# One stage for head norm and long convolutions with a product on GpSimd, HGRN states beside the projections, and full 128-row matmuls

## The reference, cut to what matters

```python
z = v
for order, gate in enumerate((x1, x2)):
    z = gate * fft_long_conv(z, two_sided(filt[:, order, 0], filt[:, order, 1]), skip[order])
```

```python
o_inter = jnp.einsum('bhck,bhkv->bhcv', qx * jnp.exp(bx), S)
S_new = jnp.exp(b_last[:, :, 0, :])[..., None] * S + jnp.einsum('bhsk,bhsv->bhkv', kx * jnp.exp(b_last - bx), vx)
o = rms_norm_2(o, out_norm) * jax.nn.silu(g.reshape(B, T, HG_HEADS, HG_DV))
```

## Time and profile before

| | |
|---|---|
| runs (us) | 4213.64, 4215.24, 4210.41; median 4213.64 |
| the profiled execution (us) | 4211.26, of which 4209.5 are the traced span |
| mean granted TensorE clock | 0.93 |
| PE busy | 89% of the span |
| DVE, ACT, POOL busy | 49%, 21%, 34% |

### The profile page before, as it was taken

The page is one execution under the profiler, slowest core; times in us unless marked ns, Lnnn a source line. Parts: engine busy times, 40 slices in busy tenths (PEclk is TensorE's granted clock), DMA queues, the critical chain, the costliest instruction groups (busy, mean ns, idle before and its releaser), DMA issues. The chain is left out here.

```text
span 4209.5 us, 45870 instructions
## 1 busy us (share of the span) xinstructions
PE 3750.4 (89%) x18394; PEld 2959.2 (70%) x18394; DVE 2054.6 (49%) x3022; ACT 872.7 (21%) x1689; POOL 1418.6 (34%) x615
## 2 busy tenths in 40 slices
PE   7897888999989889868999898878999888888998
PEld 2683567888878588746878466757887566667887
DVE  4796443223456356654233377753133477653132
ACT  2213412100021333301100344511000243501001
POOL 1321043235553100005455222235445222144444
PEclk8998789999999799988999899989999899989999
DMA  4444212212122000103322221123322221123332
GB/s 160 140 141 156 90 40 71 66 56 66 61 62 79 23 1 1 61 0 90 100 91 80 72 70 46 36 65 90 96 89 71 83 55 46 30 80 90 95 95 70
DMA packets 400355, 306.83 MB, mean 73 GB/s; under 512 B 11228, under 2 KB 367783, under 8 KB 399560
## 3 DMA queue, kind: packets, MB, share of 16 engines
q1 hardware_dynamic: 398040, 303.37, 23.4%
q10 hardware_dynamic: 2095, 0.44, 0.1%
HBM read 297.48 MB, written 6.29 MB: 72 GB/s over the span
## 5 line engine op out<-in xcount | busy, mean ns | idle before, releaser
L400 POOL TENSOR_TENSOR low<-raw,high 128x1024 fp32r<-128x1024 f32 (+1 forms) x437 | 1062.9, 2433 | 1390.4 <-DVE high L331 1390.4
L460 PE MATMUL scores<-high 128*128 128x512 f32 (+1 forms) x2496 | 962.4, 386 | 118.4 <-POOL low L400 102.7
L460 PE MATMUL scores<-low,high 128*128 128x512 f32 (+1 forms) x2496 | 948.7, 380 | 0.0
L460 PE MATMUL scores<-high,low 128*128 128x512 f32 (+1 forms) x2496 | 946.4, 379 | 0.0
L331 DVE CAST high<-raw 128x1024 fp32r<-128x1024 f32 (+1 forms) x437 | 417.3, 956 | 689.2 <-PE scores L460 376.4
L460 PE MATMUL bank<-high 128*128 128x512 f32 (+1 forms) x1760 | 648.4, 368 | 3.4 <-POOL low L400 3.4
L460 PE MATMUL bank<-low,high 128*128 128x512 f32 (+1 forms) x1760 | 647.9, 368 | 0.0
L460 PE MATMUL bank<-high,low 128*128 128x512 f32 (+1 forms) x1760 | 647.2, 368 | 0.0
L460 PEld LDWEIGHTS scores<-high 128*128 128x128 f32 x2496 | 482.3, 193 | 224.3 <-POOL low L400 111.0
L460 PEld LDWEIGHTS scores<-high,low 128*128 128x128 f32 x2496 | 480.5, 193 | 89.8
L460 PEld LDWEIGHTS scores<-low,high 128*128 128x128 f32 x2496 | 482.3, 193 | 86.1 <-issue 0.5
(11 more groups left out here) (575 smaller groups left out, 4358.3 us busy)
## 6 DMA issues: line engine op xcount, KB each, us to landing
raw<-in_mlp_w SPq DMA_DIRECT2D x128, 512.0 KB, 4.0
raw<-in_w_in SPq DMA_DIRECT2D x76, 512.0 KB, 3.8
ring<-in_ada_w SPq DMA_DIRECT2D x32, 1024.0 KB, 7.2
raw<-in_w_gate SPq DMA_DIRECT2D x44, 512.0 KB, 3.8
raw<-in_w_up SPq DMA_DIRECT2D x44, 512.0 KB, 3.7
raw<-in_w_down SPq DMA_DIRECT2D x40, 512.0 KB, 3.3
mix<-in_ada_w SPq DMA_DIRECT2D x16, 1024.0 KB, 6.7
raw<-in_od_w_in SPq DMA_DIRECT2D x29, 512.0 KB, 3.7
```

What stands on the lines that cost most here:

```text
L400: pool.tensor_tensor(tile(low, u), tile(raw, u), tile(high, u).bitcast(F32), ALU.subtract)\
L460: mm = pe.matmul(out(p), stationary, moving, start=(k0 + k == 0 and i == 0), stop=(k0 + k == job.kc - 1 and i == len(pairs) - 1))
```

## The change

1. **hyena** becomes one stage. The 512 channels are cut in two halves, and with two orders this gives four steps k of 256 channels. PE's order is written out: turn(0), the sums of the head norm, transform(0), turn(1), transform(1), transform_back(0), turn(2), two spreads of the norm, transform(2), two more, transform_back(1), turn(3), transform(3), transform_back(2), transform_back(3). DVE does, for each k, join(k), multiply(k, 0), skip_and_gate(k-1), multiply(k, 1), with the head norm's scaling behind k = 1. `long_convolution` is gone.
2. Inside it, for each k and each group of frequencies f, **GpSimd makes one of the four products** (sine spectrum by sine filter, 128x512), DVE the other three.
3. **HgrnStates** is a side of `products`: exponentials and decays at unit 0, the chain over chunks, the squares and their sums behind unit 1, the reciprocal and the spreads at unit 2, scaling and gate at unit 3. The update of the first chunk is a copy and needs no state matmul. `w_proj_a` uses banks 6 and 7 alone. `w_proj_b`'s activations are split when the gated heads are there, at the end of unit 3 (`ready`).
4. The sums and spreads of all head norms, and those of `delta_features`, use **all 128 columns and rows**; `hy_hid` and `hy_w3` of the prologue get 128 rows, the lower 64 cleared by DVE. `ones` becomes a broadcast column of `picker`.

```diff
+        def lead(i):
+            job = jobs[raws[i][1]]
+            return 1 if job.ready is not None else AHEAD if i else 3 if job.own_room else 1
...
-                pe.matmul(m.bank[1 + i % 4][:, 0:tn], m.ident[0:n, i:i + 1].broadcast_to([n, P]),
-                          roots[0:n, 0:tn], start=True, stop=True).then_inc(spread, 1)
+                pe.matmul(m.bank[1 + i % 4][:, 0:tn], m.ident[:, i:i + 1].broadcast_to([P, P]),
+                          roots[:, 0:tn], start=True, stop=True).then_inc(spread, 1)
...
-                    hy_hid=[HY_FFN, 2, T], hy_w3=[HY_FFN, 2048], hy_not_first=[P, 2, 4],
+                    hy_hid=[P, 2, T], hy_w3=[P, 2048], hy_not_first=[P, 2, 4],
...
+        @block.gpsimd
+        def _(pool):
+            for k in range(4):
+                pool.wait_ge(joined, 8 * (k + 1))
+                if k % 2 == 0:
+                    pool.wait_ge(filters_loaded[k // 2], 16)
+                for f in range(2):
+                    n = 2 * k + f
+                    if n:
+                        pool.wait_ge(added, 2 * n)
+                    pool.tensor_tensor(parts[:, 1, :, :], spectrum(k, f)[1], filter_of(k, f)[1], ALU.mult)\
+                        .then_inc(multiplied_by_gpsimd, 1)
...
+                dve.tensor_tensor(a, uc, fs, ALU.mult).then_inc(multiplied, 1)
+                dve.wait_ge(multiplied, n + 1)
+                dve.tensor_tensor(uc, uc, fc, ALU.mult).then_inc(weighed, 1)
+                dve.wait_ge(multiplied_by_gpsimd, n + 1)
+                dve.tensor_tensor(us, us, fc, ALU.mult).then_inc(weighed, 1)
+                dve.wait_ge(weighed, 2 * n + 2)
+                dve.tensor_tensor(us, us, a, ALU.add).then_inc(added, 1)
+                dve.tensor_tensor(uc, uc, b, ALU.subtract).then_inc(added, 1)
+                for half in (1, 0):
+                    for_even, for_odd = ((ALU.add, ALU.subtract), (ALU.subtract, ALU.add))[half]
+                    low, high = spec[:, k % 2, half, f, :], spec[:, k % 2, half, 2 + f, :]
+                    dve.wait_ge(added, 2 * n + 2 - half)
+                    dve.tensor_tensor(odd[:, k % 2, 2 * f + half, :], low, high, for_odd).then_inc(differed, 1)
+                    dve.wait_ge(differed, 2 * n + 2 - half)
+                    dve.tensor_tensor(low, low, high, for_even).then_inc(folded, 1)
...
-            hgrn_states(nc, m, q, f, b, part(40, 8), i_rows, yb)
-            head_norm(nc, m, yb, HEADS, (LAT,), columns[:, 23:24], 1.0, gate=gate)
+            states = HgrnStates(m, q, f, b, part(48, 12), last, part(40, 8), i_rows, yb, columns[:, 23:24], gate)
             products(nc, m, [
...
-                    "vector", room=halves),
+                    "vector", room=halves, banks=(6, 7)),
...
-                    room=halves),
+                    room=halves, ready=states.wait_for_heads),
...
-                    written_by=1, room=halves)], ring_tiles=3, sums=SquareSums(m, x, toks))
+                    written_by=1, room=halves)], ring_tiles=3, sides=[states], sums=SquareSums(m, x, toks))
```

More of the change, by code:

```diff
@@ L370, in _ @@
                     halve_weights(dve, u + AHEAD)
[L371 removed]
+                while 0 < ahead < len(raws) and lead(ahead) == AHEAD and raws[ahead][0] <= u + AHEAD:
                     halve_activations(dve, ahead)
                     ahead += 1
+                for side in sides:
+                    side.vector_first(dve, u)
                 for p in done_in.get(u, []):
@@ L1921, in long_convolution @@
[L1921 to L1929 removed]
+    W = 256
@@ new lines, in spread_root @@
+            def spread_root(i):
+                if i == 0:
+                    pe.wait_ge(inverted, 1)
+                    pe.wait_ge(skipped, 4)
+                if i >= 2:
+                    pe.wait_ge(scaled, i - 1)
+                pe.matmul(m.bank[4 + i % 2][:, :], m.ident[:, i:i + 1].broadcast_to([P, P]), roots[:, :],
+                          start=True, stop=True).then_inc(spread, 1)
+            turn(0)
+            for i in range(4):
+                pe.wait_ge(squared, i + 1)
+                mm = pe.matmul(m.bank[4][:, :], m.row_picker(i, P), sq[:, i, :], start=(i == 0), stop=(i == 3))
@@ L1961, in _ @@
+            act.activation(roots[:, :], m.bank[4][:, :], ACT.Sqrt, **inverse_root(P)).then_inc(rooted, 1)
+            copy_odd(0)
+            for k in range(1, 4):
+                copy_turned(k)
+                copy_odd(k)
         @block.vector
         def _(dve):
-            step = Chain(dve, chain)
-            spec_of = lambda v, half, f: v[:, half, :, :].rearrange("p (side f) n -> p side f n", f=2)[:, :, f, :]
-            def join(f):
-                for half in range(2):
-                    i = 2 * f + half
-                    dve.wait_ge(copied, i + 1)
-                    even, o = m.bank[2 * i][:, :], odd[:, i, :]
-                    dve.tensor_tensor(spec[:, half, f, :], even, o, ALU.add).then_inc(joined, 1)
-                    first, second = (even, o) if half == 0 else (o, even)
-                    dve.tensor_tensor(spec[:, half, 2 + f, :], first, second, ALU.subtract).then_inc(joined, 1)
@@ L2013, in delta_features @@
+            dve.wait_ge(rooted, 1)
+            dve.reciprocal(roots[:, :], roots[:, :]).then_inc(inverted, 1)
+            for k in range(4):
+                join(k)
+                multiply(k, 0)
+                if k:
+                    skip_and_gate(k - 1)
+                multiply(k, 1)
+                if k == 1:
+                    norm_heads()
+            skip_and_gate(3)
 def delta_features(nc, m, dtb, alog, rest, beta, g, qk, v, k_rows, v_rows, loads):
```

464 lines of the change are left out of this document (296 added, 168 removed).

## The result

| | before | changed |
|---|---|---|
| runs, median (us) | 4212.02 (4209.76 to 4215.24, 4 runs) | 4147.15 (4140.49 to 4148.37, 4 runs) |
| the profiled execution, its span (us) | 4211.26, 4209.5 | 4148.37, 4146.6 |
| mean granted clock | 0.930 | 0.942 |

The ratio is 0.9842, its 95% interval 0.9825 to 0.9859: 64.9 us gained, where the prediction said 78 and kept 4104 to 4161. The kernel before was measured beside every run, and its own median moved by some us from one time to the next, so I compare ratios: those of the experiments with the mean of the two, 0.9836. 0.001 of ratio is 4.2 us. The mean has a spread of its own, some 4 us either way.

The account below looks back on a forecast made before the run. It took PE (busy 89%) as limited by engines taking turns in the convolutions and HGRN, and by half clock in few-row stretches. Savings 18 + 36 + 9 + 3 + 12 = 78 gave 4135 us, range 4104 to 4161.

Parts of the forecast that it names:

- Convolutions: Merged hyena stage: DVE and PE work side by side, 122 us becomes 98 before GpSimd's effect; 18 saved, bounds 10 and 28.
- the cold last transform: End of the convolutions: PE, idle for 8 us, starts the last back transform at half clock and loses 2 us.
- GpSimd's term: Convolutions: GpSimd's products hold up DVE's, six of eight at 1.0 us each, costing 6; bounds 0 and 10.
- the clock's 8: Convolutions, low bound: the clock falls in each of four PE gaps, at 2 us each.
- HGRN: Each second layer: HGRN runs beside the projections, so `w_proj_b` starts earlier; 18 saved per layer, bounds 12 and 21.
- the takes of unit 0 come behind them: HGRN stage: DVE's decays meet GpSimd's weight lowering and delay these takes; 0 to 4 us lost, 2 taken.
- The rival of the exclusive port: GpSimd and DVE exclude each other: 10 lost in convolutions, 4 per HGRN layer; 70 saved, 4144 us; 22%.
- Prologue: Prologue filters with full rows: the clock rises from 0.50; 12 us saved, bounds 0 and 16.
- `delta_features`: Its spreads with full rows: 22.7 us at half clock becomes 13.5, cold start of 2.2 included; 9 saved, bounds 0 and 11.
- even head norm: The even layer's norm with full rows: 10.5 us becomes 7.4; 3 saved, bounds 0 and 4.
- few rows hold the clock: The rival denied this for prologue, `delta_features` and even head norm: their 24 us fall away, 54 saved, 4160 us; 12%.
- The slow one: Merged stages: short PE bursts keep the clock at 1.2 GHz, mean near 0.55; 54 us slower, 4267; 2%.

Follow-up runs that it names:

- experiment 1: The changed kernel with the convolutions' fourth product made by DVE instead of GpSimd: 4134.15 us, ratio 0.9811.
- Experiment 2: The changed kernel with DVE's HGRN decays put behind the takes of unit 0 instead of ahead of them: 4131.66 us, ratio 0.9809.
- experiment 5: The changed kernel measured a second time, unedited, as control: 4143.22 us, ratio 0.983.
- experiments 3 and 4: The changed kernel with few rows again, in the spreads of even head norm and `delta_features` (4155.95 us, ratio 0.9873), or in the prologue's filters (4153.93, 0.987).
- experiment 6: The changed kernel with the even layer's attention scores contracting 128 rows instead of 64, using half-zero query tiles copied by GpSimd: 4137.85 us, ratio 0.9824.

## Why the prediction was near, and what it mis-sized

- **Convolutions, 18 predicted, 17.4 measured.** The count of DVE's operations, its wait for the third spread and the cold last transform came as worked out. GpSimd's term was 6: six products at 1.0, two of them free in idle stretches. In the trace all eight cost 0.95, 7.6; none was free, because GpSimd starts on the same signal as DVE's own next operations, also after a stretch in which DVE idled. What each product saves stood in the chain's sum and not in that term. Set against it, experiment 1 shows a net loss of about 3.7 in DVE's chain and 5.7 in the stage. By the rule of the Trainium skill (SBUF — State Buffer, "Who interferes with whom") the prediction's term was 10, each block taken for a whole product of 1.26. The mechanism is what the stretched rows show; but DVE's operation comes when part of GpSimd's is over, and 0.95 was measured. The bounds of this part have no full working: 28 is added up nowhere, and 24 less the port's 10 and the clock's 8 is 6, not 10.
- **HGRN, 18 per layer predicted, 14.1 and 14.0 measured.** The failed step is "the takes of unit 0 come behind them, while unit 1 waits for banks 6 and 7: 0 to 4 us, I take 2". It was 6.4: 4.4 of wait, since the first two decays, stretched by 2.2 each, make the last end at 19.4 after the stage's first cast instead of 15.3, and some 2 of half clock after the pause, which had no place in the bounds. Experiment 2 returned 5.7 of it in each layer. All else there was in place: the chain began 6.6 late and ran for 15.1 (14.9), `w_proj_b` had its gap of 5.5 (5.7). The rival of the exclusive port named this loss with 4 of the 6.4.
- **Prologue, 12 predicted, 15.3 measured.** The step "if the clock rises only when filters follow each other, after 51" was the low bound, and the value was taken between the two. The clock was up from the second block on, at 37, and the high bound of 16 came true: transposes between full-row filters did not hold it down.
- **`delta_features` 10.0 (9), even head norm 3.6 (3).** As worked out; the cold start cost 1.35 in the first instead of the 2.2 assumed (12.7 for half of 22.7).
- **Unchanged stretches: nothing predicted, 11.5 lost in one profile, 1.5 in another.** The sum took all that lies outside the change as equal. Most of the distance between 78 and the 62.9 of the first profile is here. That it is mostly not the change's doing is argued: the second measurement gained 70.7, and the 3.8 that both profiles lose between the convolutions and HGRN are for the most part the clock behind one pause, which went either way in kernels that have the same program there (experiment 5). The kernel before has one profile only, so what chance did to it isn't known.

The parts meet their sum within 3.6 in part by luck: HGRN fell 7.9 short, and the prologue (3.3), `delta_features` (1.0) and the even head norm (0.6) made up for over half of it.

The rivals: few rows hold the clock (experiments 3 and 4), so that one falls. The slow one needed a granted clock near 0.55 in the merged stages; it was 0.80 to 0.92. The exclusive port said 4144, the nearest of all to the 4147.15 and 4143.22 measured. Its mechanism is what the rows show and experiment 1 bears out, yet its prices, 10 and 4 per layer, came out as 7.6 and 6.4, so the nearness of its number is partly luck. The 2.34 that the prediction reads as GpSimd alone had a cast of DVE's beside it, from 2785.77 on, which started second. The range's lower end, 4104, is worked out from no term.

## What to carry to other kernels

Ahead of giving DVE's work to GpSimd, look at what both read: beside an elementwise operation of two SBUF operands a product saved 0.49 and cost 0.95. In an order written out by hand, put what frees another engine's bank ahead of work that merely can start, and cast the next job's input ahead of the last takes; each was worth some 10 us here, as was taking the offloaded product back. Where PE is the bound at a granted clock of 0.50, look at the rows of its contraction first, and pad with zeros if nothing else in the stretch keeps the clock down and the few-row matmuls don't overlap each other (experiment 6).

## What was not expected of the hardware

- One instruction of GpSimd stretched DVE's neighbour by the same 0.95 whether DVE's had 512 elements (0.69 to 1.64) or 256 (0.42 to 1.38), and beside lowering of weights by 2.2 (0.69 to 2.85). Both follow what was left of GpSimd's instruction at DVE's start: 1.1 for the products, 2.3 for the lowering. The Trainium skill (SBUF — State Buffer, "Who interferes with whom") says that issue order, not shape, decides who blocks; this agrees, for the DVE operation that started 0.05 ahead of GpSimd's was not stretched.
- DVE's cast of weights, which has a single SBUF input, was stretched too: in the changed kernel the one at 2758.55 took 2.83 for 0.68, beside a lowering that ended at 2760.83. So two inputs are not needed for the loss.
- Zero rows raise the granted clock as well as filled ones (0.50 to 0.92 and 1.00 in the prologue), but not where matmuls of 2 columns fill the rest of the time (0.50 with 128 rows).
- The same pause of 3.35 or 3.36 us was followed by full clock in six of twelve profiles and by half clock, 12 records in the changed kernel, in the other six.
